# Three-branch attention: zero-padded keys over 128 rows, and exponentials that run one more unit ahead

## Chip, cores and metric

The kernel runs on one core of a Trainium2 chip. The metric is device time in microseconds (us), the median of the runs. One further execution was taken by the hardware profiler; all rows below come from that one. PE is TensorE (PEld its weight loads), DVE is VectorE, ACT is ScalarE, POOL is GpSimd, SP is SyncE.

## What is computed

The reference is two blocks over 512 tokens of width 1024 in float32. The first block repeats twice (two layers): a SwiGLU feed-forward, a mixing stage, and another SwiGLU. The second block (gated MLP, sliding attention, experts) runs once and the change does not touch it. The mixing stage has three kinds of attention; cut to what matters:

```python
# latent attention (MLA), 6 heads, scores contract over 64 + 32 = 96 dimensions
sc = (einsum('bqhd,bkhd->bhqk', qn, k_nope) + einsum('bqhr,bkr->bhqk', qp, k_pe)) * scale
p  = masked_softmax(sc, causal);  o = einsum('bhqk,bkhd->bqhd', p, v)

# three-branch attention (NSA), 6 query heads in 2 key groups of 3, contract over 64
o = g[..., 0:1] * o_cmp + g[..., 1:2] * o_sel + g[..., 2:3] * o_win
#   o_cmp: 31 compressed keys; o_sel and o_win: with 512 tokens both see every causal key
#   all three use the queries of the head and the keys of its group only

# stick-breaking attention, 4 heads, follows
```

## The kernel before

Everything is written out per engine; semaphores order the engines. The mixing stage first makes all queries, keys and values (a table `MIX`), applies rotary embeddings (`ROPES`, 13 of them), compresses keys and values, and then runs `attend` over a list of *units*.

A unit is one head, one block of 128 queries (`i` = 0 to 3) and one branch. MLA has 6 x 4 = 24 units, NSA 6 x 4 x 3 = 72 (`cmp`, `sel`, `win` in turn), 96 in each of two layers. Its keys are `w = (i + 1) * 128` columns, 31 for `cmp`. A unit goes through these steps:

- PE `scores` (L956): one float32 product into one of four PSUM tiles `score`. Its stationary operand is 128 queries, its moving operand the `w` key columns. MLA uses 96 rows of the array, NSA 64: the two key groups lie in partitions 0 to 63 and 64 to 127, and so do the queries of heads 0 to 2 and 3 to 5. A profile shows each such product as two instructions.
- DVE `maxima` (L1981 to L1985): adds the mask, takes the negated row maximum.
- ACT `exps` (L1536): exponentials into one of three buffers `probs`, with the row sum.
- DVE `normalize` (L1995 to L2003): reciprocal, and the scaling by it (in NSA by the gate too).
- PE `turns` (L965): transposes, a matmul whose moving operand is the identity matrix; up to 4 per unit.
- ACT `evac_turn` (L1549): copies them to one of two buffers `probs_T`.
- PE `values` (L977): sums probabilities times values into `acc`, on 64 columns of the array. After a head's last unit ACT copies `acc` to `o_T` (L1556, `head_out`).

PE's order is scores(n + 3), turns(n), values(n - 1). DVE's is maxima(n + 1), normalize(n). ACT's is exps(n + 1), evac_turn(n), head_out(n - 1). `exps(n)` waits until turns(n - 3) have been made, since there are three `probs`.

The tile `nk` has four key tiles of 128 partitions x 512: 0 for the keys to be compressed, 1 for `sel`, 2 for `win`, 3 for the values to be compressed. Tiles 0 and 3 are no longer read after the steps `xs_k` and `xs_v`, which stand before ropes 11 and 12 (the keys of `sel` and `win`) in `MIX`.

Of the kernel before, what the change touches and what calls it, by code (L numbers as in the profile page):

```python
# [19 lines left out]
ALU = mybir.AluOpType  # L20
ACT = mybir.ActivationFunctionType
# [4 lines left out]
P = 128  # L26
# [10 lines left out]
HD = 64  # L37
# [132 lines left out]
for _kind, _h in HEADS:  # L170
    for _i in range(TB):
        br = ["mla"] if _kind == "mla" else ["cmp", "sel", "win"]
# [22 lines left out]
def build(nc, a, out):  # L195
    with ExitStack() as ctx:
        def sb(name, shape):
            return ctx.enter_context(nc.sbuf_tensor(name, shape, F32))
# [23 lines left out]
        rt = sb("recip_tile", [P, S])  # L222
# [19 lines left out]
        gates = sb("gates", [P, TB, 18])  # L242
        gates_e = sb("gates_e", [P, TB, 18])
        vcmp = sb("vcmp", [31, 2, HD])
        kcmp_T = sb("kcmp_T", [P, 31])
        lnst = sb("lnst", [P, 4, TB])
        sinks = sb("sinks", [P, 8])
        rel = sb("rel", [32, 8])
# [29 lines left out]
        nq = view(3, S)  # L278
        nk = view(4, S)
# [79 lines left out]
        acc = [ctx.enter_context(nc.psum_tensor(f"acc{i}", [P, S], F32)) for i in range(2)]  # L359
# [47 lines left out]
        rope_ready = sem("rope_ready")  # L407
# [390 lines left out]
        def unit_info(n):  # L798

            kind, h, i, br, first, last = UNITS[n]  # L800
            blk = slice(i * P, (i + 1) * P)
            w = (i + 1) * P
            if kind == "mla":
                q, k = q6[0:96, h, blk], k6[0:96, h, 0:w]
                v = [mv[:, j, h * HD:(h + 1) * HD] for j in range(i + 1)]
            else:
                g, c = NSA_HALF(h)
                r = slice(g * HD, (g + 1) * HD)
                q = nq[r, c, blk]
                if br == "cmp":  # L810
                    w = 31
                    k, v = kcmp_T[r, :], [vcmp[:, g, :]]
                else:
                    k = nk[r, 1 if br == "sel" else 2, 0:w]
                    vt = vs if br == "sel" else vw
                    v = [vt[:, j, g * HD:(g + 1) * HD] for j in range(i + 1)]
            return dict(q=q, k=k, v=v, w=w, i=i, h=h, br=br, first=first, last=last,
                        out=slice((h % 2) * HD, (h % 2) * HD + HD), blk=blk,
                        head=(0 if kind == "mla" else 6) + h,
                        end=last and i == TB - 1, begin=first and i == 0)  # L820

        def swa_info(n):
# [7 lines left out]
                        out=slice((h % 2) * HD, (h % 2) * HD + HD), blk=slice(i * P, (i + 1) * P),  # L830
                        head=h, end=i == TB - 1, begin=i == 0)

        NSW = len(SWA_UNITS)
        U2 = DEPTH * NU

# [610 lines left out]
        def _(act):  # L1446
            fn = nc.scalar.activation
# [80 lines left out]
            def attend(l, per, u0, n_units, info, fr, fbase, head0, dest, sink):  # L1528
                def exps(n):
                    u = info(n)  # L1530
                    w, st = u["w"], n % 4
                    act.wait_ge(max_ready, at(l, per, u0 + n + 1))
                    if n >= 3 and not sink:
                        act.wait_ge(t_full, at(l, per, u0 + n - 2))
                    src = probs[:, n % 3, 0:w] if sink else score[st][:, 0:w]
                    m = fn(probs[:, n % 3, 0:w], src, ACT.Exp, bias=stats[:, 0, st:st + 1],  # L1536
                           accum_out=stats[:, 1, st:st + 1])
                    if sink:
                        m = fn(stats[:, 3, st:st + 1], sinks[:, u["h"]:u["h"] + 1], ACT.Exp,
                               bias=stats[:, 0, st:st + 1])  # L1540
                    m.then_inc(exp_ready, 1)

                def evac_turn(n):
                    u = info(n)
                    r, w = min(u["w"], P), len(u["v"]) * P
                    act.wait_ge(t_full, at(l, per, u0 + n + 1))
                    if n >= 2:
                        act.wait_ge(pv_done, at(l, per, u0 + n - 1))
                    fn(probs_T[0:r, n % 2, 0:w], turn[n % 2][0:r, 0:w], ACT.Copy).then_inc(pt_ready, 1)  # L1549

                def head_out(n):
                    u = info(n)
                    if u["end"]:
                        t = head0 + u["head"]
                        act.wait_ge(pv_done, at(l, per, u0 + n + 1))
                        fn(dest[u["out"], u["head"] // 2, :], acc[t % 2][u["out"], :], ACT.Copy  # L1556
                           ).then_inc(acc_free[t % 2], 1)

                exps(0)
                for n in range(n_units + 1):  # L1560
                    if n + 1 < n_units:
                        exps(n + 1)
                    if n < n_units:
                        evac_turn(n)
                    if n >= 1:
                        head_out(n - 1)

            def mix(l):
                for n, (name, i, ld, who) in enumerate(MIX):
                    if name == "cmp":  # L1570
                        for k in range(2):
                            act.wait_ge(gelu_pre, at(l, 2, k + 1))
                            fn(cmp_t[:, 2, :], cmp_t[:, 1, :], ACT.Exp, scale=-2 * GC).then_inc(gelu_exp, 1)
                    if who == "act":
                        act.wait_ge(acc_full, mix_full(l, n + 1))
                        if name == "cmp":
                            fn(kcmp_T[:, :], acc[n % 2][:, 0:31], ACT.Copy)
                            m = fn(vcmp.rearrange("p a b -> p (a b)"), acc[n % 2][0:31, 64:192], ACT.Copy)  # L1578
                        else:
                            t, sc = EVAC[name, i]  # L1580
                            m = fn(t, acc[n % 2][0:t.shape[0], 0:t.shape[1]], ACT.Copy, scale=sc)
                        m.then_inc(acc_free[n % 2], 1)
                    if ld is not None and ld + 2 < N_SPLIT and LAST_TICKET[ld] == n:
                        split_mix(l, ld + 2)
                    if (name, i) == ("ckv", 0):
                        act.drain()
                        fn(probs[:, :, :], lora[:, 0:3, :], ACT.Square).then_inc(lsq_ready, 1)
                    if (name, i) == ("ks", 0):
                        act.wait_ge(lssq_full, l + 1)
                        fn(et[:, 0, :], turn[0][:, :], ACT.Ln, scale=1.0 / 256, bias=eps[:, :])  # L1590
                        fn(et[:, 1, :], turn[1][:, :], ACT.Ln, scale=1.0 / 128, bias=eps[:, :])
                        act.drain()
                        fn(et[:, :, :], et[:, :, :], ACT.Exp, scale=-0.5).then_inc(lrstd_ready, 1)
                    if name == "gate":
                        taken(act, l, BM, n)
                        fn(gates_e[:, :, :], gates[:, :, :], ACT.Exp, scale=-1.0).then_inc(gate_exp, 1)
# [250 lines left out]
        def _(dve):  # L1847
            V = nc.vector
# [113 lines left out]
            def attend(l, per, u0, n_units, info, sink):  # L1962
# [40 lines left out]
                        V.tensor_scalar(pr, pr, stats[:, 2, st:st + 1], None, ALU.mult).then_inc(p_ready, 1)  # L2003

                maxima(0)
                for n in range(n_units):
                    if n + 1 < n_units:
                        maxima(n + 1)
                    normalize(n)

            def gelu_pre_ops(x, t):

# [9 lines left out]
            def mix(l):  # L2022
# [19 lines left out]
                for n, (name, i, ld, who) in enumerate(MIX):  # L2042
# [22 lines left out]
                    elif name == "rope":  # L2065
                        t, kind, _ = ROPES[i]
                        r = t.shape[0]
                        V.tensor_tensor(rt[0:r, :], ps[0:r, :], cst("sin_" + kind, rows=r), ALU.mult
                                        ).then_inc(acc_free[n % 2], 1)
                        V.tensor_tensor(t, t, cst("cos_" + kind, rows=r), ALU.mult)  # L2070
                        dve.drain()
                        if i == 6:
                            V.tensor_tensor(k6[HD:96, :, :], t[HD:96, :].unsqueeze(1).broadcast_to([32, 6, S]),
                                            rt[HD:96, :].unsqueeze(1).broadcast_to([32, 6, S]), ALU.add
                                            ).then_inc(rope_ready, 1)
                        else:
                            V.tensor_tensor(t, t, rt[0:r, :], ALU.add).then_inc(rope_ready, 1)
                        n_rope += 1
                        if n_rope == V_ROPES[1] + 1:
                            compressed(1, 1)  # L2080
                        if n_rope == N_ROPE:
                            compressed(0, 2)
# [82 lines left out]
            def route_weights():  # L2165
# [9 lines left out]
                dve.drain()  # L2175
                V.tensor_tensor(rx[:, 12, :, 9:10], rx[:, 12, :, 8:9], rx[:, 11, :, 0:1], ALU.mult)

            V.memset(eps[:, :], EPS).then_inc(eps_ready, 1)
            for c in range(KC):
                dve.wait_ge(xt_full, c + 1)  # L2180
# [407 lines left out]
```

## Time and profile before

| | us |
|---|---|
| median of 3 runs | 3416.02 |
| lowest, highest | 3407.52, 3427.22 |
| the profiled execution | 3429.36 |
| its span, first to last instruction | 3427.3 |
| its mean granted PE clock | 0.909 of full |

The granted clock is a share of full speed: 1.00 is 2.4 GHz, 0.50 is 1.2 GHz; a share between them in a stretch is a mixture of the two. The profiled execution is 13.3 us above the median.

### The profile page before, as it was taken

How to read it: one execution, taken by the hardware profiler on the slowest of the kernel's cores; microseconds unless marked ns; L12 is line 12 of the kernel's file. 1: busy time of each engine (PE TensorE's matmuls, PEld its weight loads, DVE VectorE, ACT ScalarE, POOL GpSimd, SP SyncE). 2: the span in 40 equal slices, each digit the busy share in tenths (PEclk: the TensorE clock that was granted, in tenths of full speed). 3: DMA queues.
4: the chain of work that ended last, by engine and by line, in shares of the span. 5: the costliest groups of instructions: out<-in, count | busy, mean ns of one | idle time of the engine just before them, and what ended most of it. 6: DMA issues, size and time to landing. Idle time of an engine off the chain costs nothing. (4 is left out here: it accounts for less than half of the span.)

```text
span 3427.3 us, 37239 instructions
## 1 busy us (share of the span) xinstructions
PE 3157.5 (92%) x13388; PEld 2367.1 (69%) x13388; DVE 2017.9 (59%) x2636; ACT 1114.2 (33%) x1638; POOL 207.7 (6%) x68
## 2 busy tenths in 40 slices
PE   6999899899899998999899999989997799969885
PEld 4888686555478886888686555468885667747774
DVE  5777713643277777777613543277776444547776
ACT  3222232434222223122221434331223234236665
POOL 0000000000000000000000000000000000016663
PEclk8999999766999999999998756999998889989998
DMA  5233122000133222322132000132222411259985
GB/s 153 86 105 103 45 70 61 25 1 1 42 114 102 86 98 75 101 95 98 45 74 57 25 1 1 37 104 92 98 73 61 98 54 50 74 191 335 326 323 204
DMA packets 234107, 324.17 MB, mean 95 GB/s; under 512 B 56608, under 2 KB 202024, under 8 KB 221568
## 3 DMA queue, kind: packets, MB, share of 16 engines
q1 hardware_dynamic: 227824, 309.50, 27.7%
q0 software_dynamic: 5584, 11.02, 1.2%
q10 hardware_dynamic: 576, 2.10, 0.2%
q8 instruction: 66, 1.08, 0.1%
q14 instruction: 57, 0.47, 0.0%
HBM read 316.82 MB, written 14.16 MB: 97 GB/s over the span
## 5 line engine op out<-in xcount | busy, mean ns | idle before, releaser
L1934 DVE SCALAR_TENSOR_TENSOR x_T<-acc,x_T 128x512 f32<-128x512 f32 x352 | 242.8, 691 | 206.5 <-PE acc L902 206.2
L871 PE MATMUL score<-h_hi,gate_hi 128*128 128x512 f32 x704 | 278.4, 396 | 34.4 <-DVE h_lo L1888 29.8
L1914 DVE RECIPROCAL recip_tile<-exp_tile 128x512 f32<-128x512 f32 x88 | 295.1, 3353 | 6.5
L872 PE MATMUL score<-h_lo,gate_hi 128*128 128x512 f32 x704 | 277.2, 394 | 0.0
L873 PE MATMUL score<-h_hi,gate_lo 128*128 128x512 f32 x704 | 276.7, 393 | 0.0
L871 PE MATMUL score<-h_hi,up_hi 128*128 128x512 f32 x704 | 274.1, 389 | 0.3 <-DVE up_lo L1871 0.3
L872 PE MATMUL score<-h_lo,up_hi 128*128 128x512 f32 x704 | 273.9, 389 | 0.0
L873 PE MATMUL score<-h_hi,up_lo 128*128 128x512 f32 x704 | 273.9, 389 | 0.0
L900 PE MATMUL acc<-hid_hi,down_hi 128*128 128x512 f32 x640 | 251.7, 393 | 8.7 <-DVE x_T L1934 8.7
L902 PE MATMUL acc<-hid_hi,down_lo 128*128 128x512 f32 x640 | 251.6, 393 | 0.0
L901 PE MATMUL acc<-hid_lo,down_hi 128*128 128x512 f32 x640 | 251.3, 393 | 0.0
L1454 ACT ACTIVATE up_hi<-weights 128x2048 fp32r<-128x2048 f32 x44 | 84.3, 1917 | 322.1 <-PE score L873 322.1
L871 PEld LDWEIGHTS score<-h_hi,gate_hi 128*128 128x128 f32 x704 | 134.2, 191 | 68.1 <-DVE h_lo L1888 33.9
L1454 ACT ACTIVATE down_hi<-weights 128x2048 fp32r<-128x2048 f32 x40 | 76.7, 1917 | 321.2 <-PE acc L902 321.2
L1519 ACT ACTIVATE exp_tile<-score 128x512 f32<-128x512 f32 x88 | 47.9, 595 | 367.4 <-PE score L873 367.4
L2520 POOL DMA_DIRECT2D rel_scratch<-probs x1 | 1.3, 1301 | 2651.5 <-DVE probs L2221 2651.5
L956 PE MATMUL score<-arena 64*128 64x128 f32 (+7 forms) x288 | 160.5, 653 | 0.9 <-ACT vcmp L1578 0.9
L2425 DVE TENSOR_TENSOR xg_lo<-arena,xg_hi 128x2048 fp32r<-128x2048 f32 x32 | 125.6, 3958 | 51.1 <-ACT xg_hi L1761 51.1
L873 PEld LDWEIGHTS score<-h_hi,gate_lo 128*128 128x128 f32 x704 | 134.1, 191 | 28.4
L872 PEld LDWEIGHTS score<-h_lo,gate_hi 128*128 128x128 f32 x704 | 134.2, 191 | 27.8
L871 PEld LDWEIGHTS score<-h_hi,up_hi 128*128 128x128 f32 x704 | 132.1, 188 | 28.5 <-DVE up_lo L1871 0.7
L2537 POOL TENSOR_TENSOR xd_lo<-weights,xd_hi 128x2048 fp32r<-128x2048 f32 x30 | 150.8, 5048 | 9.5 <-ACT xd_hi L1761 9.2
(377 smaller groups left out, 6664.8 us busy)
## 6 DMA issues: line engine op xcount, KB each, us to landing
weights<-in_ffn_w_gate SPq DMA_DIRECT2D x44, 1024.0 KB, 5.3
weights<-in_ffn_w_up SPq DMA_DIRECT2D x44, 1024.0 KB, 5.4
weights<-in_ffn_w_down SPq DMA_DIRECT2D x44, 1024.0 KB, 5.5
arena<-in_expert_w_gate SPq DMA_DIRECT2D x32, 1024.0 KB, 5.8
arena<-in_expert_w_up SPq DMA_DIRECT2D x32, 1024.0 KB, 6.9
weights<-in_expert_w_down SPq DMA_DIRECT2D x30, 1024.0 KB, 6.1
weights<-in_w_in SPq DMA_DIRECT2D x23, 1024.0 KB, 5.3
weights<-in_w_out SPq DMA_DIRECT2D x12, 1024.0 KB, 5.2
```

What stands on the lines that cost most here:

```text
L871: mm(ps, hi[:, kc, cols], h_hi[:, kc, :], start=kc == 0, stop=False, skip_group_check=True)
L872: mm(ps, hi[:, kc, cols], h_lo[:, kc, :], start=False, stop=False, skip_group_check=True)
L873: return mm(ps, lo[:, kc, cols], h_hi[:, kc, :], start=False, stop=kc == KC - 1, skip_group_check=True)
L900: mm(acc[c % 2][:, :], hi[:, j, cols], hid_hi[:, 2 * par + j, :], start=j == 0, stop=False)
L901: mm(acc[c % 2][:, :], hi[:, j, cols], hid_lo[:, 2 * par + j, :], start=False, stop=False)
L902: m = mm(acc[c % 2][:, :], lo[:, j, cols], hid_hi[:, 2 * par + j, :], start=False, stop=j == 1)
L956: mm(score[n % 4][:, 0:u["w"]], u["q"], u["k"], start=True, stop=True).then_inc(s_full, 1)
L1454: fn(w_hi[tile][:, :], slot[w][:, :], ACT.Copy).then_inc(w_hi_ready[w], 1)
L1914: V.reciprocal(rt[:, :], et[:, c, :])
L1934: V.scalar_tensor_tensor(x_T[:, c, :], acc[c % 2][:, :], 0.5, x_T[:, c, :], ALU.mult, ALU.add).then_inc(acc_free[c % 2], 1)
L2425: V.tensor_tensor(x_lo[t][j][:, :], x_raw[t][j], x_hi[t][j][:, :], ALU.subtract).then_inc(x_lo_ready[t], 1)
L2537: nc.gpsimd.tensor_tensor(x_lo["d"][j][:, :], x_raw["d"][j], x_hi["d"][j][:, :], ALU.subtract).then_inc(x_lo_ready["d"], 1)
```

## The change

NSA scores are formed over all 128 rows. The queries are taken with both groups' rows (`nq[:, c, blk]`: a head of group 0 above one of group 1), and the keys of each group stand in a tile of their own whose other 64 rows are zero, so that the other head's queries add nothing. `sel` takes tiles 1 and 0 of `nk`, `win` tiles 2 and 3, and `kcmp_T` gets a second half. DVE makes the two tiles in ropes 11 and 12: two 64-row additions in place of one over 128 rows, and two memsets. In `attend` of the first block ACT starts the exponentials one more unit ahead: exps(n + 2), evac_turn(n), head_out(n - 1), in MLA too. The code of DVE's maxima is rewritten as well.

```diff
-        kcmp_T = sb("kcmp_T", [P, 31])
+        kcmp_T = sb("kcmp_T", [P, 2, 31])
...
-                r = slice(g * HD, (g + 1) * HD)
-                q = nq[r, c, blk]
+                q = nq[:, c, blk]
                 if br == "cmp":
                     w = 31
-                    k, v = kcmp_T[r, :], [vcmp[:, g, :]]
+                    k, v = kcmp_T[:, g, :], [vcmp[:, g, :]]
                 else:
-                    k = nk[r, 1 if br == "sel" else 2, 0:w]
+                    k = nk[:, K_TILE[br][g], 0:w]
...
+        K_TILE = {"sel": (1, 0), "win": (2, 3)}
...
                 exps(0)
+                exps(1)
                 for n in range(n_units + 1):
-                    if n + 1 < n_units:
-                        exps(n + 1)
+                    if n + 2 < n_units:
+                        exps(n + 2)
                     if n < n_units:
                         evac_turn(n)
...
-                            fn(kcmp_T[:, :], acc[n % 2][:, 0:31], ACT.Copy)
+                            for g in range(2):
+                                r = slice(g * HD, (g + 1) * HD)
+                                fn(kcmp_T[r, g, :], acc[n % 2][r, 0:31], ACT.Copy)
...
                 maxima(0)
+                maxima(1)
+                normalize(0)
                 for n in range(n_units):
+                    if n + 2 < n_units:
+                        maxima(n + 2)
                     if n + 1 < n_units:
-                        maxima(n + 1)
-                    normalize(n)
+                        normalize(n + 1)
...
+                        elif i >= 11:
+                            own, other = K_TILE["sel" if i == 11 else "win"]
+                            V.tensor_tensor(nk[HD:P, other, :], t[HD:P, :], rt[HD:P, :], ALU.add)
+                            V.tensor_tensor(nk[0:HD, own, :], t[0:HD, :], rt[0:HD, :], ALU.add)
+                            V.memset(nk[0:HD, other, :], 0.0)
+                            dve.drain()
+                            V.memset(nk[HD:P, own, :], 0.0).then_inc(rope_ready, 1)
...
+            V.memset(kcmp_T[:, :, :], 0.0)
```

ACT at the start of `attend` in the kernel before (`probs<-score` are the exponentials of a unit, `probs_T<-turn` the evacuation of a unit's transposes; the widths 128, 256, 384, 512 are the four blocks of an MLA head):

```order
L1577 ACTIVATE kcmp_T<-acc 128x31
L1578 ACTIVATE vcmp<-acc 31x128
...
L1536 ACTIVATE probs,stats<-score,stats 128x128
...
L1536 ACTIVATE probs,stats<-score,stats 128x256
L1549 ACTIVATE probs_T<-turn 128x128
...
L1536 ACTIVATE probs,stats<-score,stats 128x384
L1549 ACTIVATE probs_T<-turn 128x256
...
L1536 ACTIVATE probs,stats<-score,stats 128x512
L1549 ACTIVATE probs_T<-turn 128x384
```

The same place on ACT in the changed kernel:

```order
L1580 ACTIVATE kcmp_T<-acc 64x31 x2
L1581 ACTIVATE vcmp<-acc 31x128
...
L1536 ACTIVATE probs,stats<-score,stats 128x128
...
L1536 ACTIVATE probs,stats<-score,stats 128x256
...
L1536 ACTIVATE probs,stats<-score,stats 128x384
L1549 ACTIVATE probs_T<-turn 128x128
...
L1536 ACTIVATE probs,stats<-score,stats 128x512
L1549 ACTIVATE probs_T<-turn 128x256
...
```

The 384-wide exponentials now stand ahead of the first unit's evacuation, not behind it, and so on through the 96 units; and the copy of `kcmp_T` is two instructions.

DVE in the last two ropes (11 and 12) of the changed kernel, where the kernel before had one 128x512 addition (its L2077) as the third instruction of each:

```order
L2074 TENSOR_TENSOR recip_tile<-acc,const 128x512
L2076 TENSOR_TENSOR arena<-arena,const 128x512
L2084 TENSOR_TENSOR arena<-arena,recip_tile 64x512
L2085 TENSOR_TENSOR arena<-arena,recip_tile 64x512
L2086 MEMSET arena 64x512
L2088 MEMSET arena 64x512
```

So each of the two ropes has three more DVE instructions. In `attend` itself the order of DVE's instructions is the same in both kernels (maxima 0, 1, normalize 0, maxima 2, normalize 1, ...), and PE's order of instructions is the same throughout.

## Rows read from the trace of the kernel before

**Rows 1.** The page's part 1: busy time, share of the span.
```profile
PE 3157.5 (92%) x13388; PEld 2367.1 (69%) x13388; DVE 2017.9 (59%) x2636; ACT 1114.2 (33%) x1638; POOL 207.7 (6%) x68
```

**Rows 2.** Windows: length, PE, PEld, DVE, ACT, POOL busy, clock, DMA; MLA, NSA, NSA.
```profile
615.60:663.05 47.45, 45.39 (x238) 28.89 (x238) 31.86 (x108) 26.27 (x82) 0.00 (x0) 0.96 0.14 45
663.05:828.21 165.16, 164.80 (x568) 93.45 (x568) 79.81 (x276) 61.53 (x217) 0.00 (x0) 0.62 0.00 1
...
1946.35:2125.21 178.86, 178.51 (x568) 100.94 (x568) 80.59 (x276) 61.52 (x217) 0.00 (x0) 0.56 0.00 1
```

**Rows 3.** Windows of two NSA heads, the second and third of layer one.
```profile
692.22:710.71 18.49, 18.49 (x97) 10.98 (x98) 13.29 (x48) 10.33 (x38) 0.00 (x0) 1.00 0.01 1
710.71:740.64 29.93, 29.81 (x97) 17.19 (x97) 13.70 (x48) 10.49 (x37) 0.00 (x0) 0.57 0.00 1
```

**Rows 4.** Windows in NSA ahead of a fall, then ahead of two rises.
```profile
711.50:714.90 3.40, 3.28 (x15) 1.68 (x14) 2.70 (x11) 2.39 (x11) 0.00 (x0) 1.00 0.00 0
769.50:772.90 3.40, 3.40 (x16) 2.78 (x15) 0.90 (x4) 0.50 (x3) 0.00 (x0) 0.50 0.00 0
...
687.60:691.00 3.40, 3.40 (x15) 2.56 (x13) 1.00 (x5) 0.94 (x3) 0.00 (x0) 0.50 0.01 2
```

**Rows 5.** Windows between clock changes, all engines.
```profile
691.00:714.90 23.90, 23.78 (x122) 13.95 (x121) 16.25 (x61) 13.76 (x50) 0.00 (x0) 1.00 0.00 1
714.90:772.90 58.00, 58.00 (x175) 33.33 (x175) 25.14 (x86) 17.60 (x62) 0.00 (x0) 0.50 0.00 1
```

**Rows 6.** Windows of the scores (L956) alone: PE and PEld busy, clock.
```profile
711.50:714.90 3.40, 1.80 (x6) 0.88 (x6) 1.00 0.00 0
769.50:772.90 3.40, 0.63 (x2) 0.50 (x2) 0.50 0.00 0
```

**Rows 7.** Windows of the transposes (L965) alone: PE and PEld busy, clock.
```profile
687.60:691.00 3.40, 1.01 (x5) 0.49 (x3) 0.50 0.01 2
```

**Rows 8.** Timeline of PE at full clock, MLA then NSA: start, us.
```profile
644.77 0.91 PE L956 MATMUL score<-arena 96*128 96x384 f32 x2
645.52 0.60 PE L965 MATMUL turn<-const,probs 128*128 128x128 f32 x4
...
697.14 0.91 PE L956 MATMUL score<-arena 64*128 64x384 f32 x2
697.98 0.44 PE L965 MATMUL turn<-const,probs 128*128 128x128 f32 x2
...
643.72 0.55 PE L965 MATMUL turn<-const,probs 128*128 128x128 f32 x3 [0.31 <-DVE probs L2003]
```

**Rows 9.** Timeline of DVE, ropes 11 and 12.
```profile
606.96 0.69 DVE L2077 TENSOR_TENSOR arena<-arena,recip_tile 128x512 f32<-128x512 f32 x1
608.77 0.69 DVE L2068 TENSOR_TENSOR recip_tile<-acc,const 128x512 f32<-128x512 f32 x1 [1.11 <-PE acc L1067]
```

**Rows 10.** Groups by form: busy us, mean ns; the tile kcmp_T: ns min/median/max.
```profile
L1912 DVE TENSOR_SCALAR exp_tile<-exp_tile 128x512 f32<-128x512 f32 x88 | 37.3, 423 | 124.5 <-ACT exp_tile L1519 124.5
L2178 DVE MEMSET eps<- 128x1 f32 x1 | 0.1, 59 | 0.8 <-PEq L2577 0.8
...
L1577 ACT ACTIVATE kcmp_T<-acc x2: 196/196/196, 615.2 to 1898.4; 128x31 f32<-128x31 f32 x2
```

**Rows 11.** Groups by form, ACT: the exponentials' read of the sum, and widest exponentials.
```profile
L1536 ACT ACTIVATION_READ_ACCUMULATOR probs<-score,stats 128x1 f32 x192 | 38.1, 198 | 0.0
L1536 ACT ACTIVATE probs<-score,stats 128x512 f32<-128x512 f32 x36 | 24.3, 676 | 0.0
```

**Rows 12.** Timeline of ACT: the ends of the first and fifth MLA head.
```profile
627.02 0.59 ACT L1556 ACTIVATE o_T<-acc 64x512 f32<-64x512 f32 x1 [0.74 <-PE acc L977]
...
656.61 0.59 ACT L1556 ACTIVATE o_T<-acc 64x512 f32<-64x512 f32 x1 [0.74 <-PE acc L977]
```

**Rows 13.** Timeline of DVE in NSA: two chained operations.
```profile
697.03 0.29 DVE L1983 TENSOR_TENSOR score<-score,const 128x128 f32<-128x128 f32 x1
...
697.40 0.56 DVE L1985 TENSOR_REDUCE stats<-score 128x1 f32<-128x384 f32 x1
```

## The prediction

> **What bounds the kernel now.** I read the page first: PE is busy 92% of the span [rows 1]. That says where to look, not what the change is worth, since a busy PE can be running at either of its clocks. So next I took windows over the two stages that the change touches, in both layers. The reader should see three things there [rows 2]. NSA takes 165.16 us in layer one and 178.86 in layer two, 344.0 together; MLA takes 47.45 in layer one. In NSA PE has almost no idle time (164.80 of 165.16), so PE bounds it and DVE (79.81) and ACT (61.53) are half idle. And the granted clock is 0.62 and 0.56 there, against 0.96 in MLA, where PE has *more* idle time (2.06 us of 47.45). NSA is thus bound by a PE that runs at 1.2 GHz for most of the stage while it is never idle.
>
> How much this costs shows in two neighbouring heads, which do the same work instruction for instruction: 18.49 us at clock 1.00, 29.93 at 0.57 [rows 3]. The longer one is not held up by anything else, its PE is busy 29.81 of it.
>
> **What takes the clock.** The clock changes inside NSA without PE pausing: 23.9 us at 1.00, then 58.0 at 0.50, with PE busy for all but 0.12 us of the first and all of the second [rows 5]. What differs is the mixture. In the 3.4 us before the fall at 714.9, scores with 64 rows take 1.80 us of PE's 3.28 [rows 4, 6]. In the 3.4 us before the rise at 772.9 they take 0.63, and the rest is transposes and values, which use 128 rows [rows 4, 6]. Before the rise at 691.0 five transposes take 1.01 us [rows 4, 7]. MLA is the same pipeline with 96-row scores and keeps its clock once it has it. I read this as: PE work on half of the rows counts for about half in whatever grants the clock. The change turns every 64-row score into a 128-row one. Whether rows that carry zeros count is the open point. The transposes speak for it: their moving operand is the identity, zero in 127 elements of 128, and the clock rose behind a stretch with five of them.
>
> The Trainium skill (TensorE: Matmul & The Clock Gate, Part 1) has the gate follow how busy PE has been recently, and names idle gaps as what throttles it. The trace does not agree here: busy 58.00 of 58.00 us at clock 0.50 [rows 5]. By that rule padding rows changes nothing; this is rival B.
>
> **The change part by part.**
>
> *NSA at full clock.* I take the measured head of 18.49 us as what a head costs when the clock holds. The padding also removes something at full clock. Behind a 96x384 score the transposes start 0.75 us after it (644.77 to 645.52), behind a 64x384 one 0.84 (697.14 to 697.98) [rows 8]. Both columns and clock are equal, so 0.09 us is what going from 64 to 128 rows costs, 12 times per head: 1.08 us. A padded head takes 18.49 - 1.08 = 17.41, twelve heads (two layers) 208.9. Saved: 344.0 - 208.9 = 135.1 us. The 0.09 is worth 13 of these, the clock 122. More rows do not cost columns, and the time of a matmul follows columns: 384 columns are 0.91 us with 96 rows and with 64 [rows 8].
>
> Does another engine become the bound at 17.41? DVE is busy 13.29 in the head at full clock and ACT 10.33 [rows 3]; between two chained DVE operations lie 0.08 us (697.03 + 0.29 to 697.40 [rows 13]), and with three such joints in each of 12 units DVE needs 13.3 + 2.9 = 16.2. It is close, and I keep up to 1 us per head (12 in all) for it in the range. DVE's order does not change; ACT's does.
>
> *ACT one unit further ahead.* In MLA PE waits for DVE's scaled probabilities now and then (0.31 us at 643.72 [rows 8]), and DVE for the exponentials before them. PE's idle time in MLA is 2.06 us in layer one [rows 2]. With the exponentials earlier it should go almost entirely: -4 us for both layers, between 0 and -4.2. In NSA PE does not wait now, so the lead gains nothing of its own; it keeps the faster PE fed. It costs something if evacuations come late: queued behind exps(n + 2) on ACT stands evac_turn(n), and values(n) and turns(n + 2) wait for that. The cover is PE's work between turns(n) and values(n), about one unit, 18.49 / 12 = 1.54 us. The widest exponentials and the read of their sum are 0.676 + 0.198 = 0.87 [rows 11], which fits. Taken at nothing.
>
> *Ropes 11 and 12.* Each has one more 64x512 addition and two memsets. An addition over 512 columns is 0.69 [rows 9]. No memset of that size is in the trace; it is bounded by one of a single column at 0.06 and an addition at 0.69, and I take the nearest SBUF operation over 512 columns, 0.42 [rows 9, 10]. With 0.1 for the drain (such a joint, rounded up [rows 13]) a rope grows by 0.69 + 0.84 + 0.1 = 1.63. These are on the path: PE's last product of the preparation and then `attend` stand behind DVE. But DVE waits 1.11 us for PE between the two ropes [rows 9], which hides that much of the first. The second copy of `kcmp_T` adds 0.20 [rows 10]. Per layer 3.26 - 1.11 + 0.20 = 2.35, together +4.7, between +1.8 and +6.9 with memsets of 0.06 and 0.69. The memset of `kcmp_T` at the start stands before DVE's first wait for data: nothing, at most 0.1.
>
> *Sum.* -135.1 - 4 + 4.7 = -134.4. The profiled execution took 3429.4, so 3295.0 by its own time. It lies 13.3 above the median of the runs. One more head at full clock (29.93 - 18.49 = 11.4 us less) would explain most of that, and then there is that much less to save: 3416 - 134.4 + 11.4 = 3293. The two ways agree to 2 us. I say 3294.
>
> **Rivals.**
>
> *A, the forecast, 0.80:* the clock holds at 1.00 through NSA. 3294, between 3270 (both idle terms gone, cheap memsets, and no lost head in the median: 3416 - 135.1 - 4.2 + 1.8 = 3278, and 8 for what I don't see) and 3312 (DVE bounds the head, dear memsets).
>
> *Partly, 0.08:* the clock still falls in some blocks. For it: the fall at 714.9 came in a stretch rich in short compressed units, and these stay. Against: MLA's stretches with a waiting PE hold it. Half of twelve heads at 1.2 GHz is 6 x 11.4 = 69 us more, 3363. The Trainium skill (same page, Part 4) says that transposes do not count as PE being busy; by it this case would be likelier. The rise behind five transposes [rows 7] is against it.
>
> *B, zeros do not count or the rows were not the cause, 0.08:* the clock stays as it is. Left are 0.09 us (at half clock perhaps 0.18) at each of 144 units, 13 to 26, the 4 of MLA, and 4.7 against: 3404 to 3391, say 3398, 0.5% below, on the edge of what can be told.
>
> *C, slower, 0.04:* ACT's new order makes values wait. exps(n + 2) waits for maxima(n + 2), which DVE makes behind normalize(n); if that runs late, evac_turn(n) is late with it, though its transposes are done. All 192 units would pay. It must eat 135 + 17 us to end slower, so it decides from 152 / 192 = 0.79 us per unit; at 0.9 us it gives 3282 + 173 = 3455. Against it: the cover of 1.54 us per unit, and four `score` tiles that let maxima run early.
>
> **How the numbers follow.** Under 0.5% (17 us) a measurement of this kernel cannot tell a change from none. A and the partial case are faster by more, and half of B: 0.92. Same: half of B, 0.04. Slower: 0.04. The range for 8 in 10 takes A with its bounds and reaches part of the way to the partial case: 3266 to 3345.
>
> **What would show it.** In the trace of the changed kernel: NSA windows with clock 1.00 and heads of 17 to 18 us, PE still busy throughout. If the clock is 0.5 to 0.6 with 128-row scores, the reading of rows is wrong (B). If the clock is 1.00 but heads take over 19 us with PE idle behind ACT's evacuation, it is the new order (C). Transposes that start 0.75 us behind a 384-column score show the 0.09. MLA heads of about 7.1 us show the lead: now four take 29.59, 7.40 each [rows 12], and 2.06 / 6 = 0.34 of it is PE's idle time. The additions and memsets in ropes 11 and 12 show the cost: 1.6 us each.

## The result, and the profile after

| | before | changed |
|---|---|---|
| median of the runs, us | 3421.56 (4 runs) | 3280.99 (4 runs) |
| lowest, highest | 3407.52, 3427.22 | 3276.52, 3286.37 |
| profiled execution: time, span | 3429.36, 3427.3 | 3280.57, 3278.7 |
| its mean granted PE clock | 0.909 | 0.946 |

The changed kernel takes 0.9596 of the time of the one before (95% interval 0.956 to 0.9632), 4.0% less. One more run of the kernel before stands beside those known at the prediction, which moves its median from 3416.02 to 3421.56.

The page's part 1 of the changed kernel, to be laid beside [rows 1]:

```profile
PE 3017.8 (92%) x13388; PEld 2310.0 (70%) x13388; DVE 2011.2 (61%) x2649; ACT 1119.3 (34%) x1640; POOL 207.8 (6%) x68
```

PE has the same 13388 instructions and the same 92%, but 139.7 us less of busy time. Its share says nothing about the gain, since the span shrank with it.

Windows of the changed kernel: MLA and NSA of layer one, one NSA head of layer one, NSA of layer two (columns as in [rows 2]):

```profile
621.48:666.12 44.64, 44.64 (x238) 29.58 (x239) 32.41 (x110) 27.52 (x85) 0.00 (x0) 0.93 0.15 48
666.12:765.70 99.58, 99.58 (x568) 64.89 (x569) 74.41 (x274) 62.41 (x216) 0.00 (x0) 1.00 0.01 1
682.94:699.76 16.82, 16.82 (x97) 10.99 (x98) 12.75 (x48) 10.58 (x37) 0.00 (x0) 1.00 0.01 1
1882.37:1981.95 99.58, 99.58 (x568) 64.89 (x569) 74.42 (x274) 62.41 (x216) 0.00 (x0) 1.00 0.01 1
```

NSA runs at clock 1.00 in both layers and takes 99.58 us in each, where it took 165.16 and 178.86 [rows 2]: 144.9 us less. The two layers now agree to the hundredth; before they differed by 13.7, since the clock fell at other places. PE has no idle time left in either stage (44.64 of 44.64, 99.58 of 99.58). A head takes 16.82 against 18.49 and 29.93 [rows 3], with DVE busy 12.75 of it and ACT 10.58: PE still bounds.

Stage by stage, each between the same two instructions in both traces (us, before then changed):

| stage | layer one | layer two |
|---|---|---|
| preparation of the mixing stage | 202.5, 207.9 | 206.4, 208.5 |
| MLA | 47.45, 44.64 | 47.57, 44.46 |
| NSA | 165.16, 99.58 | 178.86, 99.58 |
| end of `attend` to the second SwiGLU | 115.36, 115.73 | 117.37, 117.38 |

The four columns sum to -142.9 us (+7.5, -5.9, -144.9, +0.4). The rest of the program, which the change does not touch, gives -5.7; 5.3 of it lies behind the start of layer two's second SwiGLU (1184.7 to 1179.4), and no run here tells why. The span fell by 148.6. The row "end of `attend`" starts where NSA ends.

### The profile page after: what moved, and what is told of

It reads as the page before. It is cut to its first block and busy times, and to the rows that moved or that the text cites. A ratio compares the mean times of both kernels' runs of the same rounds, so it can differ in the third digit from the quotient of the medians.

```text
span 3278.7 us, 37258 instructions
## 1 busy us (share of the span) xinstructions
PE 3017.8 (92%) x13388; PEld 2310.0 (70%) x13388; DVE 2011.2 (61%) x2649; ACT 1119.3 (34%) x1640; POOL 207.8 (6%) x68
## 5 line engine op out<-in xcount | busy, mean ns | idle before, releaser
L872 PEld LDWEIGHTS score<-h_lo,up_hi 128*128 128x128 f32 x704 | 132.2, 188 | 27.4
L873 PEld LDWEIGHTS score<-h_hi,up_lo 128*128 128x128 f32 x704 | 132.2, 188 | 27.3
```

Source lines behind the costliest of these rows:

```text
L872: mm(ps, hi[:, kc, cols], h_lo[:, kc, :], start=False, stop=False, skip_group_check=True)
L873: return mm(ps, lo[:, kc, cols], h_hi[:, kc, :], start=False, stop=kc == KC - 1, skip_group_check=True)
```

## The experiments

Two theories at the start. **Theory 1**, mine: the rows that a score uses decide the clock, and zeros count like data; the ACT lead is worth a few us in MLA and nothing in NSA. **Theory 2**: ACT's lead is what matters, since it takes away PE's last short waits, and the clock would hold with 64 rows too. Each experiment keeps everything but its edit. The kernel before was run again beside each group, with medians of 3418.7, 3410.8 and 3425.2; ratios are against those.

**Padding without the lead.** From the changed kernel:

```diff
                 exps(0)
-                exps(1)
                 for n in range(n_units + 1):
-                    if n + 2 < n_units:
-                        exps(n + 2)
+                    if n + 1 < n_units:
+                        exps(n + 1)
```

> Padded keys, but the exponentials in their old order (exps(n + 1) ahead of evac_turn(n)). Theory 1, the 128-row scores bring the clock back by themselves: clock 1.00 in the three-branch stage, its heads 16.8 us as with the whole change, and only the latent heads go back from 6.81 to 7.40 us, 12 x 0.59 = 7: 3288 us. Theory 2, the lead of the exponentials keeps PE dense enough and so keeps the clock: clock 0.6 in the three-branch stage and about 3410 us.

Measured: 3298.68 us (3291.45 to 3300.11), ratio 0.9643 (0.9579 to 0.9707). NSA is at clock 1.00 throughout, as theory 1 has it; its time of 3288 was 11 us too low. A window of one of its heads:

```profile
686.42:703.69 17.27, 17.15 (x97) 11.00 (x97) 12.89 (x48) 10.36 (x37) 0.00 (x0) 1.00 0.01 1
```

Padding alone brings the clock. But a head is 17.27 (the next 17.41), not 16.82, with PE idle 0.12. Where the 0.45 us lies can be seen in the timeline of PE, in the short first block of the head. First this kernel:

```profile
688.65 0.41 PE L956 MATMUL score<-kcmp_T,arena 128*128 128x31 f32 x2
689.18 0.30 PE L965 MATMUL turn<-const,probs 128*31 128x128 f32 x1
689.41 0.43 PE L977 MATMUL acc<-probs_T,arena 128*64 128x128 f32 x2
```

Then the changed kernel at the same place:

```profile
685.03 0.41 PE L956 MATMUL score<-kcmp_T,arena 128*128 128x31 f32 x2
685.27 0.28 PE L965 MATMUL turn<-const,probs 128*31 128x128 f32 x1
685.48 0.43 PE L977 MATMUL acc<-probs_T,arena 128*64 128x128 f32 x2
```

The transposes come 0.53 us after the compressed score without the lead and 0.24 with it: PE makes its products in the same order in both kernels, and what these transposes need are the scaled probabilities (DVE's `probs`, the one wait of PE that the profile names in NSA there, 0.2 us). So it is the chain from exponentials to scaling that is late. The unit ahead of it is late by another 0.15. In the other three blocks of the head both kernels run alike to 0.01 us. So the lead is worth 0.45 to 0.59 a head in NSA (0.77 in the last head of a layer), 6.9 us over both layers, and 6.5 in MLA. MLA and NSA of both layers together are 13.4 us shorter with it (301.7 against 288.3). The medians differ by 17.7; the remaining 4 are of the size by which untouched stages differ between executions.

**The lead without padding.** The kernel before with the new loop of `exps`:

> The kernel before with the exponentials one more unit ahead and nothing else. Theory 1: three-branch clock stays at 0.56 to 0.62, latent heads 6.81 us, so 3421 - 7 = 3414 us. Theory 2: clock near 1.00 and 3300 us or less.

Measured: 3341.28 us (3341.03 to 3379.49), ratio 0.9774 (0.971 to 0.9838). This misses theory 1's number widely: the lead alone gives 77 us by the medians, 66 by the means. The five runs lie apart (3341.03, 3341.08, 3341.28, 3360.17, 3379.49), about 20 us at a time; the profiled one took 3360.17. Windows of its first two NSA heads in layer one:

```profile
664.84:693.87 29.03, 29.03 (x97) 16.43 (x97) 13.38 (x48) 10.66 (x37) 0.00 (x0) 0.59 0.00 1
693.87:712.31 18.44, 18.44 (x97) 10.98 (x98) 13.20 (x48) 11.02 (x38) 0.00 (x0) 1.00 0.01 1
```

The first is at the low clock for most of it, then come four at 18.44 each, where the kernel before fell in its third head. NSA as a whole is at 0.84 and 0.68, against 0.62 and 0.56. A head at full clock is 18.44 against 18.49, so but for 5.7 us in MLA the gain is the clock's. In the 3.4 us before the fall the kernel before had 0.12 us of idle PE [rows 4]; that is a wait which the lead removes. It is not in every fall: of the nine in NSA of the kernel before, six come behind a stretch with such a wait, and three (at 807.1, 2042.7 and 2104.1) behind one in which PE was never idle. So that the lead keeps the clock is shown; that it does so through these waits alone is not. Theory 1 in its strict form falls, and so does theory 2: with 64-row scores the clock still falls, PE busy 29.03 of 29.03.

**Data in place of zeros.** The other group's 64 rows hold real keys, not zeros. The scores of `sel` and `win` mix two groups, so the output is another one:

```diff
-        K_TILE = {"sel": (1, 0), "win": (2, 3)}
+        K_TILE = {"sel": (1, 1), "win": (2, 2)}
...
-                        elif i >= 11:
-                            own, other = K_TILE["sel" if i == 11 else "win"]
...
```

> Scores over 128 rows, but sel and win take the unpadded key tile of both groups, so that no half is zero; the two ropes are those of the kernel before. The scores of sel and win then mix the two groups: that part of the computation is changed. Theory 1 (what counts is that the instruction spans 128 rows, whatever the rows carry): clock 1.00 as with zeros, three-branch heads 16.82 us, and the time falls by the padding's cost in the ropes, 2 x 2.3 = 4.6 us, to 3276 us. Rival (zeros count less than data): a difference in the clock or in the heads beyond those 4.6 us.

Measured: 3657.37 us as a whole, which cannot be compared: with the other values the tokens go to more experts (256 in place of 128 of each of the products at L1357), and the program takes 1554.8 us from layer two's second SwiGLU on in place of 1179.4. The stage in question can be compared. A window of one NSA head:

```profile
684.06:700.88 16.82, 16.82 (x97) 10.99 (x97) 12.80 (x48) 10.60 (x37) 0.00 (x0) 1.00 0.00 1
```

16.82 with data, 16.82 with zeros, clock 1.00 in both, PEld equal. Whether the extra rows of `sel` and `win` hold zeros makes no difference that the trace shows, to the clock or to the time. (The extra rows of `cmp` are zero in both.)

**How much padding is needed.** Four kernels pad a part only. Three edits on the changed kernel; the first two leave one branch at 64 rows, the third pads `cmp` alone:

```diff
# compressed at 64 rows
-                    k, v = kcmp_T[:, g, :], [vcmp[:, g, :]]
+                    r = slice(g * HD, (g + 1) * HD)
+                    q, k, v = nq[r, c, blk], kcmp_T[r, g, :], [vcmp[:, g, :]]
# sel at 64 rows
+                    if br == "sel":
+                        r = slice(g * HD, (g + 1) * HD)
+                        q, k = nq[r, c, blk], nk[r, K_TILE[br][g], 0:w]
# sel and win at 64 rows (cmp padded only)
-                    k = nk[:, K_TILE[br][g], 0:w]
+                    r = slice(g * HD, (g + 1) * HD)
+                    q, k = nq[r, c, blk], nk[r, K_TILE[br][g], 0:w]
```

> The changed kernel, with only the scores of the compressed branch (31 keys) back on 64 rows. Theory 1: they stream few columns, so the clock stays at 1.00, and each of the 48 units pays what going between 64 and 128 rows costs: 0.14 us by the two traces (18.49 - 16.82 over 12 units), so heads of 16.82 + 4 x 0.14 = 17.4 us and 3281 + 6.7 = 3288 us. Rival, every 64-row score takes some of the clock: clock below 0.9 in the stage and over 3300 us.

> The changed kernel with the scores of the sel branch back on 64 rows; cmp and win stay on 128. Half of the score columns are then on half of the rows. Theory 1 (rows times time decides, and 64-row scores alone are what pulls it down): the clock still holds at 1.00, heads are 16.82 + 4 x 0.11 = 17.3 us (0.11 per unit is what the cmp branch on 64 rows cost), 3281 + 12 x 0.45 = 3286 us. Rival, each 64-row score of hundreds of columns drops the clock: stage clock of 0.8 or less, 3330 us or more.

> The changed kernel with only the compressed branch on 128 rows, sel and win on 64. Theory 1: the wide scores decide, so the clock falls in some heads as it does with the lead alone; a head at full clock takes 18.44 - 4 x 0.11 = 18.0 us, a head with a fall about 29; 3320 to 3380 us with runs that differ by tens of us. Rival, the short units are what pulls the clock down: clock 1.00 and 12 heads of 18.0, 3281 + 12 x 1.2 = 3295 us in every run.

After the third of these came out far from theory 1's number, the same kernel was run in the old order of exponentials:

> Only the compressed branch on 128 rows, as in the run where that held the clock, but with the exponentials in their old order, so that PE waits now and then (17.34 against 16.82 us a head when all is padded). Theory 1a: the clock of the half-padded stage hangs on PE's density as well as on rows, and these waits bring falls back: heads of 18.5 and of some 29 us, 3330 to 3400 us. Theory 1b: the padded short units alone hold it: clock 1.00, heads of 18.0 + 0.5 = 18.5, 3297 + 12 x 1.1 = 3310 us.

One row for each, NSA's clock in layers one and two, an NSA head at full clock, the median and its ratio:

| 64-row units in a head of 12 | ACT lead | clock | head | median | ratio |
|---|---|---|---|---|---|
| 12 (kernel before) | no | 0.62, 0.56 | 18.49 | 3421.56 | 1 |
| 12 | yes | 0.84, 0.68 | 18.44 | 3341.28 | 0.9774 |
| 8 (`sel`, `win`) | no | 0.85, 0.82 | 18.30, 18.16 | 3349.68 | 0.9808 |
| 8 (`sel`, `win`) | yes | 1.00, 1.00 | 18.00 | 3296.82 | 0.9655 |
| 4 (`sel`) | yes | 1.00, 1.00 | 17.41 | 3289.83 | 0.9637 |
| 4 (`cmp`) | yes | 1.00, 1.00 | 17.27 | 3287.36 | 0.9616 |
| 0 | no | 1.00, 1.00 | 17.27, 17.41 | 3298.68 | 0.9643 |
| 0 (changed) | yes | 1.00, 1.00 | 16.82 | 3280.99 | 0.9596 |

The clocks are those of each kernel's profiled execution, the medians those of all its runs. With `cmp` or `sel` alone at 64 rows theory 1's 3288 and 3286 were within 4 us. The window of a head with `cmp` at 64 rows, then of one with `sel`:

```profile
683.15:700.42 17.27, 17.27 (x97) 11.28 (x98) 12.93 (x48) 10.68 (x38) 0.00 (x0) 1.00 0.00 1
```

```profile
681.96:699.37 17.41, 17.41 (x97) 10.85 (x97) 13.02 (x48) 10.88 (x37) 0.00 (x0) 1.00 0.00 1
```

The window of a head with `sel` and `win` at 64 rows and the lead:

```profile
684.14:702.14 18.00, 18.00 (x97) 10.71 (x98) 13.10 (x48) 10.94 (x38) 0.00 (x0) 1.00 0.01 1
```

Two heads of the kernel with the same padding in the old order:

```profile
704.07:722.37 18.30, 18.18 (x97) 10.77 (x97) 13.09 (x48) 10.52 (x37) 0.00 (x0) 1.00 0.01 1
740.52:769.44 28.92, 28.81 (x97) 16.35 (x98) 13.79 (x48) 10.51 (x38) 0.00 (x0) 0.59 0.00 1
```

PE is idle for 0.12 and 0.11 us in the two heads of the second kernel and not at all in the first. Two things follow.

First, rows and waits act together. Padding only the compressed units, 31 columns each, holds the clock if ACT leads and does not if it doesn't. All units padded hold it even with the waits. I had said of the third kernel 3320 to 3380 by theory 1; the rival's 3295 was right.

Second, the heads at full clock price the switch from 64 to 128 rows without any change of clock. `cmp` at 64 rows costs (17.27 - 16.82) / 4 = 0.11 us per unit, `sel` (17.41 - 16.82) / 4 = 0.15, `sel` and `win` (18.00 - 16.82) / 8 = 0.15. All twelve: 0.45 + 1.18 = 1.63, and the kernel with all at 64 rows and the lead has 18.44 - 16.82 = 1.62. The sizes add up.

**Rows, or only a shorter head.** In the table the clock holds in every kernel whose head takes 18.00 us or less and falls in every one at 18.16 or more. Padding shortens the head too. So the table alone would also fit another theory, for which no run was made: that the clock follows how tightly PE's products come one after another, and rows matter only through that. A pair of stretches in the traces speaks against it, and the 8-row products further down do so more cleanly. This one is from the kernel with padding but without the lead, at the place in a head that [rows 4] shows ahead of the fall at 714.9:

```profile
704.60:708.00 3.40, 3.22 (x15) 1.67 (x14) 2.75 (x12) 2.27 (x11) 0.00 (x0) 1.00 0.00 0
```

Both stretches hold the same three scores (256, 31 and 384 columns) and as many PE instructions. PE is busy for 3.22 us here and was for 3.28 there, so it was fed no more tightly here. With 128 rows the clock stays at 1.00 to the end of NSA, with 64 it fell.

**The same rule elsewhere.** The changed kernel still loses its clock for 20 us in the second block, at 2671.9, with PE never idle. That stretch holds 16 products that use 8 rows (a bias added by a product), in the profile 32 instructions. In the next kernel the 8 rows became 128, the others zero:

```diff
+        bs_pad = sb("bs_pad", [P, P])
...
-                    m = mm(ps[:, b * P:(b + 1) * P], cst("group_rows", 8, i * P, (i + 1) * P), bs[:, :],
+                    m = mm(ps[:, b * P:(b + 1) * P], cst("group_rows", P, i * P, (i + 1) * P), bs_pad[:, :],
...
+            V.memset(bs_pad[:, :], 0.0)
...
+            V.tensor_copy(bs_pad[0:8, :], bs[:, :])
```

> The changed kernel, and in the second block the 16 bias products with 8 rows (the spatial gate) made over 128 rows, 120 of them zero, at the price of one more 128x128 memset and an 8x128 copy. In the changed kernel's trace the clock goes to 0.50 at 2671.9 us, behind a few of these products with PE never idle, and stays there 20.5 us. Theory 1 (rows of the array in use, zeros counted): that fall goes, 10 us less in that stage, some 2 us more for not going between 8 and 128 rows: 3269 us. If zero rows or the row count do not matter: no change, 3281 us.

Measured: 3275.38 us (3273.66 to 3278.74), 5.6 us below the changed kernel's median where 12 were expected. First the window in the changed kernel:

```profile
2671.90:2692.40 20.50, 20.50 (x83) 13.01 (x80) 6.18 (x11) 2.19 (x4) 0.00 (x0) 0.50 0.01 2
```

The line of the products (duration in ns: lowest, median, highest; first and last start; rows*columns of the array):

```profile
L1234 PE MATMUL acc<-bs,const x32: 270/417/578, 2668.9 to 2687.3; 8*128 8x128 f32 x32
```

Then, in the kernel with 128 rows, the window over the same stretch:

```profile
2671.90:2692.40 20.50, 20.50 (x130) 13.97 (x127) 10.78 (x23) 5.41 (x15) 0.00 (x0) 1.00 0.08 26
```

And its line of the same products (one further down in the code):

```profile
L1235 PE MATMUL acc<-bs_pad,const x32: 275/326/377, 2670.4 to 2682.5; 128*128 128x128 f32 x32
```

Clock 1.00 in place of 0.50, and 130 PE instructions in the same 20.5 us in place of 83. The sliding attention, from its first score to its last, goes from 147.2 us to 138.2. Nothing of the change's own stage was touched, so this is an independent case of the same effect. In all ten traces in which these products use 8 rows the clock falls about 3 us behind the first of them, and in none of the three in which they use 128.

This case also leaves no room for the theory of the shorter head. Here are the first 3 us of these products in the changed kernel, ahead of the fall:

```profile
2668.90:2671.90 3.00, 3.00 (x26) 1.96 (x24) 0.12 (x1) 1.52 (x5) 0.00 (x0) 1.00 0.97 324
```

And the first 3 us of them in the kernel with 128 rows:

```profile
2670.40:2673.40 3.00, 3.00 (x26) 1.98 (x24) 0.09 (x1) 1.53 (x5) 0.00 (x0) 1.00 0.96 323
```

PE runs the same 26 instructions at full clock in both, never idle, each group of one bias product and its neighbours in 0.78 us with 8 rows and 0.79 with 128. Only the rows of the bias products differ, and the clock falls in the first and stays in the second.

**Both, with the sliding attention's scores padded too.** Its 64-row scores take their keys from two zero-padded tiles, laid into two tables that are dead by then:

```diff
-            return dict(q=q2[r, c, i * P:(i + 1) * P], k=k2[r, lo * P:(i + 1) * P],
+            return dict(q=q2[:, c, i * P:(i + 1) * P], k=k2p[g][:, lo * P:(i + 1) * P],
...
+        k2p = [cst("cos_mla"), cst("sin_mla")]
...
+            V.memset(k2p[0][HD:P, :], 0.0)
+            V.memset(k2p[1][0:HD, :], 0.0)
...
-                        m = fn(k2, ps, ACT.Copy)
+                        fn(k2p[0][0:HD, :], ps[0:HD, :], ACT.Copy)
+                        m = fn(k2p[1][HD:P, :], ps[HD:P, :], ACT.Copy)
```

> As with the bias products padded, and the sliding attention's 64-row scores (32 units) also over 128 rows, with zeroed halves in two key tiles. Theory 1: a further 32 x 0.11 = 3.5 us from not going between 64 and 128 rows, less 1 us for two memsets of 64x512; and the 10 us of the bias products' fall: 3266 us. If neither fall goes: 3279 us.

Measured: 3269.25 us (six runs, 3266.33 to 3272.66), 3 above theory 1's number. The line of its scores in the changed kernel:

```profile
L1246 PE MATMUL score<-arena x64: 272/376/792, 2609.4 to 2756.6; 64*128 64x256 f32 x48, 64*128 64x128 f32 x16
```

And in this one (two further down in the code):

```profile
L1248 PE MATMUL score<-const,arena x64: 273/379/795, 2609.0 to 2742.9; 128*128 128x256 f32 x48, 128*128 128x128 f32 x16
```

From the first to the last of the 64 scores: 147.2, then 133.9 us, and 4.3 of the 13.3 are beyond the step before (138.2). A score's own duration is the same.

**The changed kernel and this version side by side**, on one chip, six runs each:

> The changed kernel itself, for a comparison on the same chip with the version that pads the second block too: 3281 us.

> The version with the bias products and the sliding attention padded as well, beside the changed kernel on the same chip: 12 us less than it, 3269 us; the sliding stage was 133.9 us against 147.2. If the difference seen before was the chip's, both take the same.

Measured: 3282.28 us (3278.25 to 3285.61) and 3270.91 (3268.70 to 3273.42). The ranges do not meet; the means are 3282.60 and 3270.96, so the version with both pads is 11.6 us faster than the changed kernel, 0.35%. It is the fastest of all that ran, at 0.9562 (0.9522 to 0.9603) of the kernel before.

## Why the prediction was right, and where it was not

3294 was forecast and 3280.99 measured. By the profiled executions the sum was -134.4 and -148.6 came. Case A is what happened. Step by step:

- **"What takes the clock": rows.** Right as the cause of this change's gain, shown by padding alone (clock 1.00 in NSA, 120.0 us below its own runs of before) and by the 8-row products elsewhere. Right too that zeros count: data in the same rows gives the same 16.82. It was not the whole. I had the 0.12 us of idle PE before the fall in front of me [rows 4] and set it aside. Lead alone is worth 77 us and padding alone 120, the two together 138 to 141: each protects the same clock, and the effects overlap rather than add. That the rows count by themselves, and not only through a shorter head, rests on the pair of stretches above and on the 8-row products.
- **NSA, -135.1.** Measured -144.9, the largest miss of the sum. The term was built of heads of 17.41; they are 16.82, which is 12 x 0.59 = 7.1 us, and the last head of each layer is 1.35 shorter again (15.47, no following scores), 2.7. The step that was mis-sized is "0.09 us is what going from 64 to 128 rows costs". It is 0.11 to 0.15. I measured only from the score to the transposes, and that part was right (0.75 us after the padded score, below). I overlooked that the group of transposes itself got shorter.
- **"In NSA the lead gains nothing of its own."** Wrong. It is worth about 0.5 us per head once the padding is there, at the short first block. With the other error this hid itself: a head with padding alone comes out at 17.27 and 17.41, my number, with 1.6 saved by rows and some 0.5 lost to waits that a faster PE has begun to see. The measured "no wait" of a slower PE was no evidence for a faster one.
- **MLA, -4 for both layers.** Measured -2.8 and -3.1. PE's idle time of 2.06 did go to 0.00, and heads went from 7.40 to 6.81, 0.59 each, where I expected 7.1. The idle time that the profile lists was less than what the late probabilities cost, as in NSA, where 0.12 us of idle time went with 0.45.
- **DVE as the bound, 16.2 per head.** Did not occur: DVE is busy 12.75 in 16.82 and PE has no idle time. A need of 16.2 would still fit into 16.82, so whether that figure is right no run here tells.
- **Ropes 11 and 12, +2.35 a layer.** Layer two, where the clock was equal in both traces, gives +2.26 from rope 8 to the first score (17.76 to 20.02). The sum is right by two errors that cancel. A rope grew by 1.93, not 1.63: the memset is 0.485 where I took 0.42, and the drain and starts take the rest. The first rope is hidden wholly and not for 1.11 us only. The second copy of `kcmp_T` costs 0.33. Below, DVE in rope 12 of layer two:

```profile
1828.82 0.69 DVE L2074 TENSOR_TENSOR recip_tile<-acc,const 128x512 f32<-128x512 f32 x1 [0.71 <-PE acc L1067]
...
1830.18 0.69 DVE L2084 TENSOR_TENSOR arena<-arena,recip_tile 64x512 f32<-64x512 f32 x1
1830.89 0.68 DVE L2085 TENSOR_TENSOR arena<-arena,recip_tile 64x512 f32<-64x512 f32 x1
1831.63 0.48 DVE L2086 MEMSET arena<- 64x512 f32 x1
1832.32 0.48 DVE L2088 MEMSET arena<- 64x512 f32 x1 [0.20 <-issue]
```

  DVE waited 2.64 us for PE ahead of this rope before and 0.71 now: the 1.93 by which rope 11 grew came out of that wait. In layer one preparation grew by 5.4; some 3 of it are not the ropes but a clock that fell some 9 us earlier there. Padding is not its cause: it fell at 587.0 to 590.0 us in every other trace too, also with the lead alone (590.0), whose ropes are those of before (598.9). Why the kernel before fell later no run tells.
- **Rival B** (zeros don't count, 3398) is out by the clock of 1.00 and by the run with data. The rule of the Trainium skill that it rested on (TensorE: Matmul & The Clock Gate, Part 1: busy time decides) may hold for a part here, since the lead, which takes 0.12 us of waits away, raised NSA's clock from 0.62 and 0.56 to 0.84 and 0.68; it is not enough, since a PE busy 29.03 of 29.03 us stood at 0.59.
- **The partial case** (3363) did not come. Its form is that of the kernel with the lead alone (3341) and of the one with only `cmp` padded in the old order (3350).
- **Rival C** is out: PE has no idle time at all in MLA and NSA, so no value waits for a late evacuation.
- **The median.** I placed the kernel before at 3416 and subtracted 11.4 us less than the profiled sum would. With the fourth run it is 3421.56, so by the medians 140.6 us came off where 122 were forecast. The forecast of 3293 that follows lies 12 high, mostly the NSA term (9.8), the MLA term (1.9) and the untouched stages, less the extra 3 of preparation.

The misses of size mostly pointed one way: the cost of a row change was too small, the lead in NSA was put at nothing, and the forecast for the median held back 11.4 us. Luck had a small part: the baseline was 5.5 us too low, which brought the forecast nearer to what was measured.

What stays open: how rows and idle time are weighed against each other, why the lead keeps the clock where PE was not idle before a fall, and why the kernel with the lead alone varies by 20 us from run to run. The table shows which mixtures hold here, not a law.

## What to carry to other kernels

When a busy PE stands at half clock, look at the rows that its matmuls use: padding the contraction of short products to 128 rows with zeros cost no columns here and gave 3.6% alone and 4% with the lead, and a part of the matmuls was enough once PE's last small waits were gone. Test each half of such a change alone before crediting one of them, since both guard the same clock and their gains overlap. And when a change makes the bounding engine faster, its waits have to be read anew: "it does not wait now" was true only of the slow one.

## What the hardware showed that was not expected

**A weight load that starts early.** Timeline of PE in the changed kernel, beside [rows 8]:

```profile
687.26 0.91 PE L956 MATMUL score<-arena 128*128 128x384 f32 x2
688.01 0.38 PE L965 MATMUL turn<-const,probs 128*128 128x128 f32 x2
688.32 0.65 PE L977 MATMUL acc<-probs_T,arena 128*64 128x128 f32 x4
```

Timeline of PEld there:

```profile
687.69 0.14 PEld L965 LDWEIGHTS turn<-const,probs 128*128 128x128 f32 x1
```

PEld in the kernel before, at the place of [rows 8]:

```profile
697.98 0.20 PEld L965 LDWEIGHTS turn<-const,probs 128*128 128x128 f32 x2 [0.55 <-issue]
```

Behind a 128-row score the weights of the first transpose load at 687.69, while the score's products still run, 0.32 us before the transpose. Behind a 64-row score the same load starts only with the transpose, at 697.98. That is the 0.15 us: 0.84 to 0.75 from score to transposes, and 0.37 to 0.31 from these to the values. The Trainium skill (TensorE: Matmul & The Clock Gate, Part 3, The mechanism) says that PE pulls a weight load ahead of running matmuls when its rows don't conflict or when it goes to the background buffer. Pulling ahead is what the trace shows; that it stops behind a product on half of the rows the page does not say.

**Eight rows are enough to lose the clock.** 16 products on 8 rows, in a stretch where PE is busy 20.50 of 20.50 us, go with a clock of 0.50; on 128 rows of mostly zeros the same stretch is at 1.00.

**A memset of 64 x 512** float32 on DVE is 0.485 us, against 0.69 for an addition of the same size.
